# Six first units, not four, multiplied raw on the input's first half, with the level masks made by GpSimd and ScalarE

## The reference

```python
c_act = jax.nn.silu(c)
for l in range(DEPTH):
    mod = (c_act @ ada_w[l] + ada_b[l])[:, None, :]
    sh1, sc1, g1, sh2, sc2, g2 = jnp.split(mod, 6, axis=-1)
    h = rmsnorm(x, norm_mix_w[l]) * (1.0 + sc1) + sh1
    x = x + g1 * hybrid_mixer(h, lb_all[l], w_in[l], ...)
...
def hybrid_mixer(h, lb, w_in, ...):
    proj = h @ w_in
    (a_b, a_c, a_h, b_q, b_f, b_i, b_g, c_u, c_v, gate_a, gate_b, gate_c) = jnp.split(proj, split_idx, axis=-1)
    y_a = short_conv_mixer(a_b, a_c, a_h, conv_w) @ w_br_a
    y_b = hgrn2_mixer(b_q, b_f, b_i, b_g, lb, hgrn_norm_w) @ w_br_b
```

## Time and profile before

| | us |
|---|---|
| median of 3 runs | 1507.74 |
| lowest and highest | 1505.51, 1510.28 |
| profiled execution, span | 1505.1 |
| TensorE busy | 1490.6 (99%) |
| VectorE busy | 1299.7 (86%) |
| ScalarE busy | 959.8 (64%) |
| GpSimd busy | 26.7 (2%) |

### The profile page before, as it was taken

How to read it: one execution, slowest core, us unless ns; L and a number is a source line. 1 busy time by engine, 2 the same in 40 slices (tenths; PEclk the granted TensorE clock), 3 DMA queues, 4 the chain that set the end, 5 groups by cost and what they waited for, 6 DMA issues and landing times.

```text
span 1505.1 us, 24325 instructions
## 1 busy us (share of the span) xinstructions
PE 1490.6 (99%) x8505; PEld 1311.0 (87%) x8505; DVE 1299.7 (86%) x1529; ACT 959.8 (64%) x1107; POOL 26.7 (2%) x44
## 2 busy tenths in 40 slices
PE   8999999999999999999999999999999999999997
PEld 7999888999999999888988888888888888888886
DVE  7999787777775799787799999999999999999998
ACT  3636445444544535444588888887878878788885
POOL 0000000000000000000010000000000000000100
PEclk9999999999999999999999999999999999999999
DMA  9956498388995646588399999999999999999993
GB/s 349 341 173 221 151 331 293 103 291 297 377 410 193 210 154 218 174 291 306 109 398 397 410 394 404 372 379 409 363 392 369 382 406 364 393 369 379 411 393 139
DMA packets 210458, 470.89 MB, mean 313 GB/s; under 512 B 16156, under 2 KB 93140, under 8 KB 210388
## 3 DMA queue, kind: packets, MB, share of 16 engines
q1 hardware_dynamic: 206624, 457.27, 83.0%
q0 software_dynamic: 3488, 12.59, 2.1%
q10 hardware_dynamic: 276, 0.09, 0.0%
HBM read 454.69 MB, written 15.21 MB: 312 GB/s over the span
## 4 chain that ended last, share of the span: by engine, by line
PE 94%; DVE 3%; DMA 1%; ACT 0%; issue 0%; DVEq 0%; SPq 0%; ACTq 0%
PE psU L671 68%; PE psA L671 24%; DVE split L2046 1%; PE psA L1155 1%; DMA raw<-in_ada_w_dram 1%; PE psU L1115 0%; DVE adacc L1655 0%; PE psU L1068 0%; PE psA L747 0%; ACT split L1254 0%; DVE adacc L1652 0%; DVE work L1655 0%; DVE merged L1677 0%; DVE xT L2027 0%; DVE work L1652 0%
## 5 line engine op out<-in xcount | busy, mean ns | idle before, releaser
L1254 ACT ACTIVATE split<-raw 128x1024 fp32r<-128x1024 f32 x750 | 781.8, 1061 | 300.0 <-PE psU L671 134.3
L2046 DVE TENSOR_TENSOR split<-raw,split 128x1024 fp32r<-128x1024 f32 x528 | 617.2, 1221 | 22.8 <-ACT split L1254 10.4
L671 PE MATMUL psU<-split,yS 128*128 128x512 f32 x2448 | 564.6, 390 | 0.1
L671 PEld LDWEIGHTS psU<-split,yS 128*128 128x128 f32 x2448 | 458.0, 188 | 94.9 <-DVE split L2046 0.8
L671 PE MATMUL psU<-hS,split 128*128 128x256 f32 x2688 | 331.0, 285 | 0.1
L1507 DVE TENSOR_TENSOR split<-raw,split 128x1024 fp32r<-128x1024 f32 x222 | 264.2, 1219 | 77.3 <-ACT split L1254 76.5
L671 PEld LDWEIGHTS psU<-hS,split 128*128 128x128 f32 x2688 | 326.3, 193 | 1.5 <-issue 1.2
L671 PE MATMUL psA<-split,hidE 128*128 128x512 f32 x1056 | 246.0, 392 | 0.0
L671 PEld LDWEIGHTS psA<-split,hidE 128*128 128x128 f32 x1056 | 196.4, 188 | 40.2
L671 PE MATMUL psU<-split,hS 128*128 128x512 f32 x720 | 168.4, 391 | 0.0
L671 PEld LDWEIGHTS psU<-split,hS 128*128 128x128 f32 x720 | 134.3, 188 | 28.0 <-DVE split L1507 0.4
(11 more groups left out here) (267 smaller groups left out, 824.5 us busy)
## 6 DMA issues: line engine op xcount, KB each, us to landing
raw<-in_moe_w_dram SPq DMA_DIRECT2D x496, 512.0 KB, 5.8
raw<-in_w_in_dram SPq DMA_DIRECT2D x116, 512.0 KB, 6.0
raw<-in_ada_w_dram SPq DMA_DIRECT2D x96, 512.0 KB, 7.8
raw<-in_ffn_w_dram SPq DMA_DIRECT2D x66, 512.0 KB, 8.6
raw<-in_moe_w_dram SPq DMA_DIRECT2D x64, 256.0 KB, 6.2
raw<-in_w_o_dram SPq DMA_DIRECT2D x16, 512.0 KB, 5.5
token_rows<-sc SPq DMA_DIRECT2D x11, 512.0 KB, 13.0
raw<-in_w_br_a_dram SPq DMA_DIRECT2D x8, 512.0 KB, 6.6
```

The lines of the kernel that those rows point to most:

```text
L671: return pe.matmul(o, a, b, start=start, stop=stop, skip_group_check=True)
L1254: return act.activation(o, i, ACT.Copy)
L2046: TTN(split[:, slot, 1, :], raw[:, (RAW0 + n) % RAW, :], split[:, slot, 0, :].bitcast(F32), ALU.subtract).then_inc(s_lo, 1)
```

## The change

- `START_UNITS` covers f, q and ab: six units are multiplied raw on the first half of h. Two more whole pieces go to rows 4 and 5 of `work`, loaded behind the last of the 16 start pieces, and the two split pieces of ab for the first half of h are gone. The raw work has `half_section(1, 1)` behind its third unit and `half_section(0, 1)` behind its fifth; the 11 fill matmuls ahead of the first split piece are gone, and `FILL_CHUNK` goes from 6 to 4.
- Six units need six banks: the two f units take the `psA` pair of the event ("half", 0), and a semaphore `s_f0` tells when ScalarE has emptied them.
- The levels 0 and 1 now stand behind the six units, in front of the first ac unit; before, they stood behind ab 0 and ab 1. `turn_gating` comes behind six units too.
- GpSimd makes the level triangles in `levels`: two memsets of 128 x 1024 and 28 linked affine selects of 64 elements in a partition. ScalarE copies them to the byte masks, ahead of its copy of `rstd`. VectorE's 19 instructions on masks shrink to two copies of the identity, and SP no longer waits for them.
- VectorE's product 5 moves from ahead of `modulate_half(1, 0)` to behind the first two chunks, and TensorE's `row_factors` to ahead of the second `direct_piece`.

```diff
-START_GROUPS = HEAD_GROUPS[:2]
+START_GROUPS = HEAD_GROUPS[:3]
 START_UNITS = [(0, g, j) for g in START_GROUPS for j in range(2)]
+EVENT_UNITS = START_UNITS[:2]
+WHOLES = (0, 1, 2, 6, 4, 5)
...
-FILL_X, FILL_SCALE, FILL_SUM, FILL_SHIFT, FILL_CHUNK = 6, 5, 4, 3, 6
-FILL_LOWER = 11
+FILL_X, FILL_SCALE, FILL_SUM, FILL_SHIFT, FILL_CHUNK = 6, 5, 4, 3, 4
...
-WHOLE_AT = {len(START) // 2 - 1 + (0, 2, 4, 6)[n]: [n] for n in range(4)}
+WHOLE_AT = {len(START) // 2 - 1: [0], len(START) // 2 + 1: [1], len(START) // 2 + 3: [2], len(START) // 2 + 5: [3],
+            len(START) - 1: [4, 5]}
...
                     for n in WHOLE_AT[pos]:
-                        if n == 0:
-                            sp.wait_ge(s_rows, 1)
...
+            for back in range(2):
+                link(pool.memset(levels[back], 0.0))
+            for j in range(1, NLEV - 1):
+                h = 2 ** (j - 1)
+                n = P // (2 * h)
+                grid = ones[:, 0:n * h].rearrange("p (n h) -> p n h", h=h)
+                for back in range(2):
+                    part = levels[back][:, j * P:(j + 1) * P].rearrange("p (n c h) -> p n c h", c=2, h=h)[:, :, 1 - back, :]
+                    link(pool.affine_select(out=part, in_=grid, compare_op=ALU.is_ge, fill=0.0, base=-back * h,
+                                            pattern=[[-2 * h, n], [0, h]], channel_multiplier=1))
+                    link(pool.affine_select(out=part, in_=part, compare_op=ALU.is_ge, fill=0.0, base=back * h + h - 1,
+                                            pattern=[[2 * h, n], [0, h]], channel_multiplier=-1))
             pool.memset(sc[:, :, :, :], 0.0).then_inc(s_sc, 1)
+            pool.tensor_tensor(stored[:, :], ones[:, 0:1], ones[:, 0:1], ALU.add).then_inc(s_tri, 1)
...
                     fill(bank, FILL_SHIFT)
+                    row_factors(bank)
                     direct_piece(1)
-                    row_factors(bank)
                     half_section(0, 0)
                     start_units()
...
                 if l == 0:
                     turn_gating()
+                    for lev in range(2):
+                        level(l, lev)
+                    lev = 2
...
                 std(vst[:, 2:4], vst[:, 0:2], D).then_inc(s_rms, 1)
+                act.wait_ge(s_tri, 1)
+                for back, dst in ((0, masks), (1, masks_back)):
+                    copy(dst[:, 1:NLEV - 1, :].rearrange("p j t -> p (j t)"), levels[back][:, P:1024]).then_inc(s_masks, 1)
                 bank, _ = event((0, "norm1"))
                 copy(rstd[:, :], bank[:, 0:T]).then_inc(s_eA, 1)
...
-                start_products([5])
                 modulate_half(1, 0)
                 dve.wait_ge(s_eA, emptied(EVENTS, EVENT_AT[(0, "norm1")], "A"))
                 start_chunks(0, range(2))
+                start_products([5])
+                start_chunks(0, range(2, 4))
                 modulate_half(0, 0)
-                start_chunks(0, range(2, 4))
                 lower_bounds()
                 start_products(range(6, 14))
+                dve.wait_ge(s_masks, 2)
                 modulate_half(1, 1)
```

More of the change, by code:

```diff
@@ L108, in unit_plan @@
         for g in HEAD_GROUPS:
-            plan += [((l, g, j), "A" if g in ("f", "ab", "ac", "i", "u") else "D") for j in range(2)]
-            if l == 0 and g == "q":
+            plan += [((l, g, j), "A" if g in ("f", "ab", "ac", "i", "u") else "D") for j in range(2)
+                     if (l, g, j) not in EVENT_UNITS]
+            if l == 0 and g == START_GROUPS[-1]:
                 plan += [(("wt", 0), "D"), (("wt", 1), "D")]
@@ L156, in unit_signals @@
     signal = {}
-    for key, _ in UNITS:
+    keys = [key for key, _ in UNITS]
+    first = keys.index(START_UNITS[2])
+    for key in keys[:first] + EVENT_UNITS + keys[first:]:
         kind = key[1] if len(key) == 3 and isinstance(key, tuple) else key[0]
@@ L458, in program, with f_bank @@
         s_yfirst = sem("expert_first_half_ready")
+        def f_bank(j):
+            return psA[2 * (EVENT_AT["half", 0] % 2) + j]
         def accumulator(s):
@@ L818, in start_units @@
             def start_units():
[L820 to L825, removed]
+                open_event(("half", 1))
+                banks = [f_bank(j) for j in range(2)] + [open_unit(key) for key in START_UNITS[2:]]
+                fill(banks[2], FILL_CHUNK)
+                pe.wait_ge(s_eD, emptied(EVENTS, EVENT_AT["half", 0], "D"))
+                for n in range(len(START_UNITS)):
                     pe.wait_ge(s_whole[n], 16)
@@ L833, in start_units @@
                     if n == 2:
-                        open_event(("half", 1))
                         half_section(1, 1)
-                half_section(0, 1)
-                pe.wait_ge(s_eD, emptied(EVENTS, EVENT_AT["half", 0], "D"))
-                fill(psA[2 * (EVENT_AT["half", 0] % 2)], FILL_LOWER)
-                for n, key in enumerate(keys):
+                    if n == 4:
+                        half_section(0, 1)
+                for n in range(len(START_UNITS)):
                     w = next_split()
@@ L1515, in unit @@
                     upto = used + 3
+                if key[0] == "wt":
+                    upto = used + 2
                 if used:
@@ L1536, in _ @@
             link(dve.memset(items[:, :], 0.0))
-            dve.wait_ge(s_const, 9)
-            xor = work[:, 0, 0:P].bitcast(I32)
-            above, below = work[:, 1, 0:P], work[:, 1, P:2 * P]
-            link(TTN(xor, iotas[:, 0, :], iotas[:, 1, :], ALU.bitwise_xor))
-            link(TTN(above, iotas[:, 1, :], iotas[:, 0, :], ALU.is_gt))
-            link(TTN(below, iotas[:, 0, :], iotas[:, 1, :], ALU.is_gt))
-            settle()
-            for j in range(8):
-                link(STT(work[:, 2, j * P:(j + 1) * P], xor, float(2 ** j), above, ALU.is_ge, ALU.mult))
-                link(STT(work[:, 3, j * P:(j + 1) * P], xor, float(2 ** j), below, ALU.is_ge, ALU.mult))
+            dve.wait_ge(s_const, 7)
             link(dve.tensor_copy(masks[:, 0, :], ident[:, :]))
             link(dve.tensor_copy(masks_back[:, 0, :], ident[:, ::-1]))
-            settle()
-            for row, dst in ((2, masks), (3, masks_back)):
-                ins = TTN(dst[:, 1:8, :].rearrange("p j t -> p (j t)"), work[:, row, 0:7 * P], work[:, row, P:8 * P], ALU.subtract)
-                if row == 2:
-                    link(ins)
-            ins.then_inc(s_rows, 1)
             dve.wait_ge(s_cact, 1)
```

33 lines of the change are left out of this document (20 added, 13 removed).

## The result

The changed kernel is slower: 1515.45 us median of 6 runs (1514.23 to 1518.60) against 1507.12 us (6 runs, 1505.51 to 1510.28), ratio 1.0056 with a 95% interval of 1.0044 to 1.0068. That is 8.4 us, where 2.9 were forecast; the time lies just outside the range, and slower by over 0.3% is what came. The profiled execution had a span of 1517.1 us and took 1518.60, 3.2 above the median of its kernel.

What follows compares the result with a forecast made beforehand. TensorE, at 94% of the span, bounds the kernel, with VectorE a second bound just below. VectorE's 2.9 us delay added to the span of 1505.1 gives 1508.0; the median's extra 2.6 makes 1510.6, range 1505.5 to 1515.0.

Steps and rivals of the forecast that it cites:

- rstd: Start: complete at 18.65 us against 19.16, since product 4 comes 0.5 us earlier; rests on masks not being late.
- rstd to first raw unit: Start: two chunks 0.83, product 5 to shift 2.73, shift to raw matmul 1.24, 0.06 between; 4.86 us in all.
- six raw units, two half sections: TensorE at the start: 14.95 for four units and one half section, plus two units of 3.53 and 0.82; 22.8 us.
- six split pieces: TensorE behind the raw units: 2.91 us a piece, six instead of four, 17.45 us to the gating transposes.
- transposes to first ac unit: TensorE from the gating transposes to the first ac unit: 3.35 us, as now; that unit begins at 67.15 by TensorE alone.
- late at the second half of v: TensorE at the low part awaited at 108.88: 2.9 us behind, as VectorE is, with nothing given back later.
- the price of a select: GpSimd's 28 selects at the start: 0.21 us each plus 0.08 link, 8.1 us together; triangles ready at 14.5, needed by 16.4.
- the upper end: GpSimd's selects at 0.29 us with a 0.24 link: 14.8 us, triangles ready at 21.2, costing 4.8 us.
- The first rival: Start: GpSimd's selects contend with VectorE's products, triangles at 18.9, rstd 2.5 us late; +5.4, 1513.1 us; chance 0.34.
- Slower by more needs late masks: Slower by over 0.3% (4.5 us) needs three quarters of late masks (0.34) or noise on the forecast; chance 0.31.
- the new wait: VectorE waits for gating transposes behind six units; TensorE waits 2.0 us for a low part, second ac unit at 75.75.
- The second rival: Gating transposes: VectorE keeps up, so TensorE alone counts; -0.4 us, 1507.3 us; chance 0.15.

Runs made afterwards that it cites:

- masks by VectorE: Changed kernel with the level masks made by VectorE again, GpSimd's selects and ScalarE's copies removed, six raw units kept; 1510.17 us, ratio 1.0040.
- The reversed one: Changed kernel with GpSimd's 28 selects in reverse order of levels, blocks of 64 tokens first; 1513.68 us in a single run.
- b1_masks_pool_alone: Kernel before, four raw units kept, with only the masks from GpSimd and ScalarE as in the change; 1512.11 us, ratio 1.0047.
- a1_masks_behind: Changed kernel with ScalarE's wait for GpSimd and its two mask copies moved behind the chunks of h's first half; 1510.15 us, ratio 1.0032.
- a4_filled_wait: Changed kernel with 27 unused filling products on TensorE behind the second direct piece, ahead of the half section; 1519.77 us, ratio 1.0083.
- k1_masks_behind_fill: a1_masks_behind with 8 more fill matmuls ahead of row_factors (11 for 3); 1509.67 us over 12 runs, ratio 1.0021.
- k2_product5_ahead: k1_masks_behind_fill with product 5 back ahead of the chunks and the last two chunks behind the shift's read; 1508.08 us, ratio 1.0002.

## Why the prediction was wrong

Step by step, forecast against the changed kernel, and against the two in which the masks are not late. Starts in us; "rstd" is its end:

| step | forecast | changed | masks by VectorE | copies behind, filled |
|---|---|---|---|---|
| rstd | 18.65 | 23.65 | 19.15 | 18.26 |
| rstd to first raw unit | 4.86 | 5.99 | 4.81 | 4.81 |
| six raw units, two half sections | 22.85 | 22.42 | 22.39 | 22.40 |
| first split piece | 46.35 | 52.06 | 46.35 | 45.47 |
| six split pieces | 17.45 | 17.45 | 17.47 | 17.46 |
| transposes to first ac unit | 3.35 | 3.47 | 3.47 | 3.47 |
| TensorE waits up to the second ac unit | 2.0 | 1.72 | 1.72 | 1.72 |
| late at the second half of v | 2.9 | 8.8 | 3.1 | 2.2 |

**The failing step is the price of a select:** "I take half way between the durations, 0.21, and the link of 0.08". The measured mean from start to start is 15.15 / 28 = 0.54, above even the upper bound of 0.53 (0.29 and 0.24), and for another reason than that bound had: the link is 0.07, but the duration goes up to 0.65 with the pattern, and to 0.86 beside a product. I had priced by the printed 128 x 64, and the rows for it were selects over a plain run of 128 elements. The shape that the trace lacked was not the count but the number of pieces. The code showed it: `pattern=[[-2 * h, n], [0, h]]` with n of 64 at h of 1. That term was 7.0 us too small; 1.9 were slack, and 5.0 came through to rstd. The range was short of its own sum as well: 1510.6 and the 4.8 of the upper end are 1515.4, not the 1515.0 that it gives for it. That the time came as near to it as it did is luck: the bound was made of other terms than those that were measured, and had none for the clock.

**The first rival had the right mechanism, but only half of the cause.** It said that selects wait beside VectorE's two-input products, and put the triangles at 18.9. They came at 21.56: by the account above the waiting cost 3.3 us, and the patterns 3.8. Either alone would have made them late: 16.4 was the need, and they would have been ready at some 18.3 with the patterns alone and at 17.8 with the waiting alone (worked out from the rows, not run). The products were not stretched: the eight of them from 8.53 to 15.59 keep 0.75. By the Trainium skill (SBUF — State Buffer, Who interferes with whom) whichever of the two starts first holds the pair of ports to its end; the trace agrees on GpSimd's side (in all eight cases the product had begun first, and selects of 0.26 to 0.46 took 0.64 to 0.86). Of VectorE's side the changed kernel shows nothing for products. The reversed one has a select that began first, by 0.01 us (spans on GpSimd are rough), and the product behind it took 0.77; but a one-input instruction at 16.70, behind the select of 0.66 at 16.63, took 0.67, where it takes 0.29 in the changed kernel (at 16.77):

```profile
9.18 0.29 POOL L626 TENSOR_SCALAR_AFFINE_SELECT work<-ones 128x64 f32<-128x64 f32 x1
9.19 0.77 DVE L1660 SCALAR_TENSOR_TENSOR work<-raw,cact,work 128x512 f32<-128x512 f32 x1 [0.19 <-DMA raw<-in_ada_w_dram]
...
16.70 0.67 DVE L1700 TENSOR_SCALAR work<-ones,vst 128x128 f32<-128x128 f32 x1
```

**No term had the clock.** rstd to the first raw unit was 4.86 in the forecast and 4.81 in both kernels at full clock; in the changed one 5.99. So the low clock behind the 6.5 us wait cost 1.2, of which the half section has 0.9 (1.97 and not 1.10). It adds up: 3.1 (the kernel with VectorE's masks) + 4.5 (rstd at 23.65 and not 19.15) + 1.2 = 8.8. "Slower by more needs late masks" was right in kind, and at 0.34 too small a chance for a term whose upper bound alone reached past the need.

**What was right.** The six raw units and the new wait, to within half a microsecond in each row of the table; the loads of raw pieces hidden; VectorE idle until the second shift is read (5.59 us, at 48.94); no time given back behind 109. The forecast's 0.5 for an earlier rstd (VectorE free of mask work) is right too, and more: 18.26 where nothing waits for the masks, 0.9 earlier than the 19.16 of before. What came with it wasn't in the forecast: `row_factors` now stands ahead of the second direct piece, whose 1.90 us filled that time before, and TensorE waits 1.75 us for the row factors. (The times at which the last two whole pieces are needed, 38.9 and 43.3 in the prediction, are 38.5 and 42.8 by its own sum; nothing hangs on it.) The second rival, VectorE keeping up, falls: the waits ahead of the ac units are there in all three.

**What stays open.** By the ratio, the time of the kernel with VectorE's masks is 6.0 us over the kernel before (4.1 to 8.0); its trace shows 3.1. A fall of the clock at its start doesn't explain it: the recorded execution has none there, and took 1509.98 us at a mean granted clock of 0.995; two more of the five, the median of 1510.17 among them, have the same clock and lie within 0.2 us. The difference is rather in what the kernel before was given in that session: 0.995 to 0.998, with a median of 1505.22, where this one had 0.990 to 0.995. Over all sessions the kernel before has 19 runs at 0.995, with a median of 1507.28; the three at 0.995 are 2.7 to 2.9 above that, close to the trace. So the 6.0 is in part the luck of the clock, and the 7.1 of `b1_masks_pool_alone`, measured against the same runs, may be too. Nor is it shown why the wait for the row factors brings the clock down in one execution and not in another: the changed kernel, `a1_masks_behind` and `a4_filled_wait` are alike up to the end of that wait, which is 1.75 or 1.76 us in all three, and the clock behind it was 1.00, 0.51 and 0.53. TensorE was busier ahead of it where the clock held (3.97 us of the 4 from 6 to 10, against 2.87 and 3.01), but in the kernel with VectorE's masks it was busy for 2.03 there, waited 1.72, and the clock held too.

## What to carry to other kernels

An instruction whose shape the trace hasn't is priced by its pattern, not by its element count: if the row nearest to it has another number of pieces, the upper bound has to allow for the pieces, and a bound above the slack means that the moved work must be taken out of the critical engine's queue first. Here the two copies stood ahead of rstd for no reason; behind the hS copies no one waited for the late selects (`k1_masks_behind_fill`: rstd complete at 18.26). And a wait of TensorE can cost more than its length where the clock falls in it: of two kernels with the same work, the one with the wait filled was 3.1 us ahead in its trace, a difference that their times are too noisy to confirm.

## What the runs showed of the hardware

- GpSimd's select of 64 elements: 0.24 us as one piece, 0.65 as 64 pieces of one element, in either order of the levels. Adding the pieces up, a further one costs about 0.0065 us, (0.65 - 0.24) / 63.
- VectorE's one-input instructions did get longer beside GpSimd's memset, though the two-input ones didn't (0.28 and 0.29 at 3.29 to 4.57 in the kernel before, beside the memset of `sc`, as behind it). The two casts of the identity at 2.90 took 0.94 and 0.86 us beside the memset of `work`, where they take 0.22 each when GpSimd is idle (at 7.26 in the kernel before); a product of 4 elements took 1.40 beside the memset of `sc`:

```profile
2.81 0.94 POOL L619 MEMSET work<- 128x1024 f32 x1
2.90 0.94 DVE L1564 CAST masks<-ident 128x128 uint8<-128x128 f32 x1 [1.69 <-POOL ov L616]
3.04 0.86 DVE L1565 CAST masks_back<-ident 128x128 uint8<-128x128 f32 x1
```

in the changed kernel, and in `k2_product5_ahead`:

```profile
21.46 1.40 DVE L1578 TENSOR_SCALAR lbs<-lbs 128x4 f32<-128x4 f32 x1
21.46 1.38 POOL L630 MEMSET sc<- 128x1536 f32 x1
```

- The granted clock also falls where TensorE is busy nearly or quite throughout (24.44 and 25.00 us of 25), and not in the same place in every execution. A window of the kernel before, and then one of the changed kernel; in either stretch the other kernel had 1.00:

```profile
465.00:490.00 25.00, 24.44 (x177) 23.94 (x176) 17.74 (x37) 11.64 (x19) 0.00 (x0) 0.86 0.27 86
```

```profile
490.00:515.00 25.00, 25.00 (x173) 25.00 (x173) 24.00 (x42) 15.13 (x21) 0.00 (x0) 0.80 0.53 173
```

The mean over an execution of the kernel before goes with its time: 0.998 at 1502.65 us and 0.992 at 1512.77. That is the spread against which a start worth 3 us has to be measured.
